# Sample attention: the turned key pages copied out of the shared PSUM bank by VectorE instead of ScalarE

## The reference

```
def _sample_attend(q, k, v, lam, past_k, past_v):
    ...
    k_all = jnp.concatenate([past_k.astype(k.dtype), k], axis=1).reshape(b, p_len + t, DIFF_HEADS, 2, DIFF_HD)
    v_all = jnp.concatenate([past_v.astype(v.dtype), v], axis=1)
    ...
def _diff_core(q, k, v, mask, lam):
    s = jnp.einsum('bqhcd,bkhcd->bhcqk', q, k).astype(jnp.float32) * (DIFF_HD ** -0.5)
    p = jax.nn.softmax(jnp.where(mask, s, NEG_INF), axis=-1)
    a = (p[:, :, 0] - lam * p[:, :, 1]).astype(v.dtype)
    return jnp.einsum('bhqk,bkhe->bqhe', a, v)
```

## Time and profile before

| | us |
|---|---|
| median of three runs (1576.26 to 1578.45) | 1576.59 |
| the profiled execution, its whole time | 1581.38 |
| its span in the trace | 1579.7 |
| PE busy | 1463.8 (93%) |
| DVE busy | 956.6 (61%) |
| ACT busy | 578.3 (37%) |

### The profile page before, as it was taken

One profiled execution on the slowest core, in us unless ns is written; L12 is line 12 of the kernel. 1 busy time (PEld: TensorE's weight loads), 2 busy tenths in 40 slices (PEclk: granted clock), 3 DMA queues, 4 the chain that ended last, 5 costly groups with the idle time before them and its releaser, 6 DMA issues.

```text
span 1579.7 us, 28049 instructions
## 1 busy us (share of the span) xinstructions
PE 1463.8 (93%) x10932; PEld 1394.9 (88%) x10932; DVE 956.6 (61%) x1825; ACT 578.3 (37%) x969; POOL 156.1 (10%) x202
## 2 busy tenths in 40 slices
PE   4899876989999999999999999997899999999997
PEld 3799774789999999999988877775899999999997
DVE  4789888556663565366765455665566635653662
ACT  3444433444341222123555344444333322221222
POOL 2000103212000000000200333220110000000001
PEclk7899987789999999999999899996899999999999
DMA  7121222114233232322322333331123323233222
GB/s 208 42 66 54 88 86 70 43 53 134 87 87 92 83 94 80 94 84 67 96 81 67 108 104 105 107 94 54 53 86 89 93 81 94 82 91 90 85 74 68
DMA packets 223088, 134.88 MB, mean 85 GB/s; under 512 B 7612, under 2 KB 216209, under 8 KB 222936
## 3 DMA queue, kind: packets, MB, share of 16 engines
q1 hardware_dynamic: 215143, 111.54, 24.5%
q0 software_dynamic: 7840, 21.89, 4.7%
HBM read 126.19 MB, written 7.85 MB: 85 GB/s over the span
## 4 chain that ended last, share of the span: by engine, by line
PE 76%; DVE 14%; ACT 5%; issue 3%; SPq 1%; DMA 1%; POOL 0%; ACTq 0%; DVEq 0%; POOLq 0%
PE acc L522 58%; PE acc L699 6%; DVE conv_out L1625 3%; PE psT L957 2%; ACT w_hi L1093 1%; DVE w_lo L1528 1%; DVE softmax_stats L2016 1%; PE psX L534 1%; PE psX L893 1%; ACT exps L1391 1%; PE psX L786 1%; PE acc L534 1%; PE psT L999 1%; SPq L415 1%; PE psX L656 1%
## 5 line engine op out<-in xcount | busy, mean ns | idle before, releaser
L522 PE MATMUL acc<-xa_hi,w_hi 128*128 128x272 f32 x1760 | 371.7, 293 | 8.4 <-DVE xa_lo L1563 8.4
L522 PE MATMUL acc<-xa_hi,w_lo 128*128 128x272 f32 x1760 | 365.9, 289 | 0.0
L522 PE MATMUL acc<-xa_lo,w_hi 128*128 128x272 f32 x1760 | 364.9, 289 | 0.0
L1093 ACT ACTIVATE w_hi<-w_raw 128x1024 fp32r<-128x1024 f32 x194 | 205.4, 1059 | 378.1 <-PE acc L522 304.2
L1528 DVE TENSOR_TENSOR w_lo<-w_raw,w_hi 128x1024 fp32r<-128x1024 f32 x194 | 237.8, 1226 | 98.9 <-ACT w_hi L1093 97.4
L522 PEld LDWEIGHTS acc<-xa_hi,w_hi 128*128 128x128 f32 x1760 | 279.0, 190 | 13.6 <-issue 11.9
L522 PEld LDWEIGHTS acc<-xa_lo,w_hi 128*128 128x128 f32 x1760 | 278.5, 190 | 0.0
L522 PEld LDWEIGHTS acc<-xa_hi,w_lo 128*128 128x128 f32 x1760 | 276.6, 190 | 0.0
L522 PE MATMUL acc<-xb_hi,w_hi 128*128 128x272 f32 x896 | 197.1, 302 | 2.0 <-DVE xb_lo L1962 2.0
L522 PE MATMUL acc<-xb_hi,w_lo 128*128 128x272 f32 x896 | 187.7, 291 | 0.0
L522 PE MATMUL acc<-xb_lo,w_hi 128*128 128x272 f32 x896 | 187.2, 291 | 0.0
(11 more groups left out here) (306 smaller groups left out, 1998.0 us busy)
## 6 DMA issues: line engine op xcount, KB each, us to landing
w_raw<-in_w_up SPq DMA_DIRECT2D x88, 512.0 KB, 3.9
w_raw<-in_w_down SPq DMA_DIRECT2D x32, 512.0 KB, 3.9
w_raw<-in_w_in_a SPq DMA_DIRECT2D x14, 512.0 KB, 4.1
w_raw<-in_w_down SPq DMA_DIRECT2D x16, 384.0 KB, 3.4
w_raw<-in_w_kv SPq DMA_DIRECT2D x12, 512.0 KB, 3.9
k_pages<-in_cache_k POOLq DMA_DIRECT2D x96, 64.0 KB, 2.1
v_pages<-in_cache_v SPq DMA_DIRECT2D x96, 64.0 KB, 1.9
w_raw<-in_w_mem_kv SPq DMA_DIRECT2D x8, 512.0 KB, 3.8
```

The costliest lines, as they stand in the source:

```text
L522: last = nc.tensor.matmul(acc[slot][:, c, 0:n], w, x[:, k, c * n:(c + 1) * n], start=(k == 0 and q == 0), stop=(k == kb - 1 and q == 2))
L1093: nc.scalar.activation(whi[:, slot % 2, :], wraw[:, slot, :], ACT.Copy).then_inc(w_hi_ready, 1)
```

## The change

The 24 copies of turned key pages, `turned_pages`, are done by DVE instead of ACT. They keep their slots. In DVE's slot they stand behind `normed` and `taken` and ahead of `maxes`. Nothing else changes: the same transposes, the same bank, the same waits.

```
-                nc.scalar.activation(kTs[:, q * 512:(q + 1) * 512], psT[:, 0, :], ACT.Copy).then_inc(turn_taken, 1)
...
-                for u in due("KT", g):
-                    turned_pages(u)
...
+            def turned_pages(u):
+                h, q = divmod(u, 4)
+                dve.wait_ge(turn_full, turn_at("KT", u) + 1)
+                if q == 0 and h:
+                    dve.wait_ge(at_S, item(h - 1, 4) + 1)
+                nc.vector.tensor_copy(kTs[:, q * 512:(q + 1) * 512], psT[:, 0, :]).then_inc(turn_taken, 1)
...
                 for n in due("O", g):
                     taken(n)
+                for u in due("KT", g):
+                    turned_pages(u)
                 for n in due("S", g):
                     maxes(n)
```

## The result

The changed kernel takes 1585.41 us (median of 5, 1584.28 to 1588.06), the kernel before 1576.59 us (5 runs, 1575.76 to 1578.45). The ratio is 1.0056 (95% interval 1.0042 to 1.0071): slower by 8.8 us. I had forecast 1581.2, slower by 4.6, inside a range of 1577.0 to 1587.0; the direction and the places were right, the size was about half of what came. 1585.41 lies inside the stated range, but above the 1578.5 to 1584 that I had given for the forecast case alone.

A forecast was written before the change was run, and what follows sets the result against it. PE, busy 93% of the span, bounds the kernel, so only its waits count. Heads 1 to 4 add 4.88 us, head 0 +0.41, head 5 -0.68: +4.6 on the median 1576.59, so 1581.2 us, range 1577.0 to 1587.0.

The forecast's parts named there:

- Price of a copy, latency: A 128x512 copy from this bank takes 692 ns on DVE, 595 on ACT; PE's turn begins 0.14 us after it.
- q2 late: In heads 1 to 4, q2's copy waits on DVE behind `normed` and O0's copy, so T1 starts 1.70 us later.
- q3 early: On DVE q3's copy follows item 3's maxima; T2 starts only 0.34 us later, getting back 1.36 of the 1.70.
- Late next, at KS: At the head's end the chain to KS starts 1.70 us late, regains 0.48; the next head begins 1.22 late.
- The swallowed rival: Room in the chain to KS absorbs the late T1; about +0.2 us in all, 1576.8 us; chance 0.17.
- Head 5: In head 5, without a projection beside it, T2 starts 0.74 us earlier, of which S4 keeps 0.68.
- q0 and q1 at nothing: Moving q0's and q1's copies to DVE costs 0; bounds minus and plus 0.69 us a head.
- The sum: Over the heads: 4.88 in heads 1 to 4, +0.41 in head 0, -0.68 in head 5, total +4.6 us.
- The clock rival: T1's new waits of about 2 us draw two to four more half-clock stretches, +3.4 to +6.8 us: 1584.6 to 1588.0; chance 0.19.
- The range: Measured time of the whole kernel between 1577.0 and 1587.0 us, to leave out 2 in 10.
- The sign that I had named for the clock: The clock case would show as a lower granted clock in the two stretches that read 0.94 and 0.83 before.

The follow-up runs named there:

- the edit on T3's copy: Changed kernel with ACT's copy of T3, in the steps of keys, ahead of the root with its table load: ratio 1.0005 to the kernel before.

## Why the prediction was right, and by how much it was not

- **Price of a copy, latency.** Right: 0.68 to 0.69 us on DVE here too, T1 0.15 us behind its end.
- **q2 late.** Right: 1.70 by the sum, T1's wait 2.15 to 2.17 (forecast 2.16), heads 0 to 1 +1.69 with q2 alone, and DVE is bound by the exponents and `normed` ahead. That order is the cause: moved ahead of `normed`, the same copy leaves T1 without a wait.
- **q3 early.** Right: T2 gets back 1.39 (1.36), q3 alone is a gain of 0.48 a head.
- **Late next, at KS.** Right: new wait of 0.5 at O2 (0.6), KS 1.03, 1.19 and 1.21 carried a head at equal clock (1.22). The swallowed rival is out, and the edit on T3's copy shows the place. Head 5: T1 to T2 takes 6.20 us where it was 8.67, so -2.47 (forecast -0.74 - 1.70 = -2.44).
- **q0 and q1 at nothing.** Nearly: +0.9 us in the stage, nothing in the time.
- **The sum, and the step that failed.** The stage is 8.0 us longer, not 4.6. Interval by interval: S0 to T1 of head 0 +1.19 (forecast +0.89), then +1.19, +2.72, +2.40, +1.21, +1.77, then -2.47 to T2 of head 5, and 0.0 to the end. The step is the clock's term, which the sum had at zero. In two heads the slow part doubled (+1.50 and +1.18 over 1.22), in heads 4 to 5 there is another +0.55, in head 0 +0.30, of which q0 and q1 are some 0.2. Together 3.5, less 0.1 of small terms: the 3.4 missing. The two doublings stand in the rows. The +0.55 is less clear: the mean clock of heads 4 to 5 rose (0.86 for 0.80), but the slow stretch met more of O4's 32 narrow matmuls, which take 6.27 us there where they took 5.03, while S2 behind them is at full rate again (0.92 us, before 1.65).
- **The clock rival** had the sign and the size right (1584.6 to 1588.0) and the mechanism wrong. It had T1's new wait draw the slow stretches. In both profiles of the changed kernel none begins behind T1 of heads 0 to 4; the stretches begin within the 32 narrow matmuls of O4 (128x4, L957) or just behind, as before the change, and last 6.8 us where two of them had lasted 3.4. Waits of 2.2 and 2.9 us at T1 did have slow stretches behind them in the kernels with T3 early (two heads of four) and with q2 copied twice (three of four), and those cost little. In the kernel with q2 alone on DVE waits of 2.15 to 2.23 us had none in four heads, so the length of the wait does not decide it alone.
- **The range** held because I had widened it for the clock and the swallowed case; the sum by itself, with its own 1578.5 to 1584, did not reach 1585.41. That much of the hit is luck. The sign that I had named for the clock, a lower figure in the stretches that read 0.94 and 0.83, came in one only: they read 0.92 and 0.86.
- **What goes with 3.4 and 6.8, and what is open.** In the fourteen profiles heads 0 to 3 have 56 slow stretches at O4. The 27 of 6.8 us begin 2.3 to 3.5 us behind the first of O4's narrow matmuls, the 29 of 3.4 us begin 3.7 to 5.6 us behind it. Before the change the four distances are 3.3, 4.5, 3.8 and 2.7 us; in the changed kernel they are 2.7, 2.6, 2.6 and 2.5 (stretches from 928.9, 966.5, 1004.0 and 1041.6 us), in its second profile 3.0 to 3.1. So in the changed kernel the stretch begins early in O4 in every head. What sets the moment at which a stretch begins stays open: no run here changed it and nothing else.

The Trainium skill's rule on banks ("Perfetto Trace Analysis", section "Optimizing Tensor Performance") speaks of overlap by rotation. Here there is one bank and no rotation, and yet 0.5 us a head came from giving q3 to the other engine, and more than that (1.7) was lost with q2: the start of the copy in each engine's queue decided, in both directions.

## What to carry to other kernels

Before a copy moves to another engine, read what stands ahead of it in that engine's order at that moment, and what that waits for: the same 24 copies on the same engine cost 8.8 us behind `normed` and gained 5.0 ahead of it. Busy shares (61% and 36%) say nothing on that. Follow the delay past the first wait that it ends, to the last wait of the period, here the copy of T3 behind a root with a table load; that place was worth 5 to 9 us more, though the change never touched it. Where the clock falls in each period, compare periods at equal clock first, and give the clock its own term.

## What the runs showed of the hardware that I had not expected

- A slow stretch in each head begins within the 32 matmuls of 128x4 (L957) or just behind them, though the records show PE busy all through the 6.8 us ahead of it (962.2 to 969.0 before). In the changed kernel 966.7 to 970.1 has a granted clock of 0.50 and 970.1 to 973.5 of 0.53. In the kernel before the stretch begins at 969.0, and 972.8 to 976.2 is at 1.00 again.

```profile
966.70:970.10 3.40, 3.40 (x16) 3.32 (x15) 1.21 (x8) 0.00 (x0) 0.00 (x0) 0.50 0.54 158
970.10:973.50 3.40, 3.40 (x15) 2.42 (x15) 1.62 (x3) 0.00 (x0) 0.00 (x0) 0.53 0.45 126
```

```profile
972.80:976.20 3.40, 3.40 (x26) 2.67 (x25) 2.17 (x8) 1.80 (x7) 0.78 (x2) 1.00 0.44 128
```

- The same kernel repeats its slow stretches from one execution to the next: two profiles of it differ by 0.05 us over the stage of 239. The pattern belongs to the kernel's timing, and a change of 1.2 us a head had 1.5 and 1.2 more attached to it in two heads out of four.
